# A bank emptied ahead of the next weights' split, rows of roots later, and a wider state-space table

## What is computed

```python
for l in range(2):
    h = h + 0.5 * swiglu(rmsnorm(h, ffn1_norm[l]), ...)          # hidden width 2816
    h = h + hybrid_mixer(rmsnorm(h, mix_norm[l]), w_in[l], ...)  # mLSTM, retention, gated delta rule
    h = h + 0.5 * swiglu(rmsnorm(h, ffn2_norm[l]), ...)
h = rmsnorm(h, final_norm)
hn = rmsnorm(h, norm1_w)                                         # second kind of block
gates, z, xbc, dt_raw, lru_x, lru_y = split(hn @ w_in)
y_ssm = mamba2_mixer(z, xbc, dt_raw, ...) @ w_out_ssm            # 4 groups of 8 heads, chunks of 128
y_lru = rglru_mixer(lru_x, lru_y, ...) @ w_out_lru               # width 1280, associative scan
h = h + (sigmoid(g_ssm) * y_ssm + sigmoid(g_lru) * y_lru) @ w_out
h = h + swiglu(rmsnorm(h, norm2_w), ...)
return rmsnorm(h, norm_f_w)
```

## Time and profile before

| | |
|---|---|
| median of 3 runs | 3571.42 us (3570.7 to 3572.22) |
| profiled execution | 3571.62 us; its span from first to last instruction 3569.5 us |
| TensorE matmuls busy | 3362.7 us, 94%, 15366 instructions |
| weight loads busy | 2724.7 us, 76%, beside the matmuls |
| VectorE busy | 1722.0 us, 48% |
| ScalarE busy | 1334.0 us, 37% |
| transfers | 288.05 MB, mean 81 GB/s |
| mean granted clock of TensorE | 0.978 |

### The profile page before, as it was taken

How to read it: one execution, slowest core, us unless ns; L and a number is a source line. 1 busy time by engine, 2 the same in 40 slices (tenths; PEclk the granted TensorE clock), 3 DMA queues, 4 the chain that set the end, 5 groups by cost and what they waited for, 6 DMA issues and landing times.

```text
span 3569.5 us, 38933 instructions
## 1 busy us (share of the span) xinstructions
PE 3362.7 (94%) x15366; PEld 2724.7 (76%) x15366; DVE 1722.0 (48%) x2415; ACT 1334.0 (37%) x1894; POOL 30.6 (1%) x62
## 2 busy tenths in 40 slices
PE   8999989899999999998989999989998998999998
PEld 6888766677888888876667788877777876778887
DVE  4443444754443444344575444455445566544443
ACT  4332335343332333233534332345444456433322
POOL 0000000000000000000000000000000000000000
PEclk9999999999999999999999999999999999999999
DMA  4233211112333233321111223321211222333332
GB/s 141 95 97 94 93 65 53 33 54 89 97 94 99 91 99 92 98 90 59 59 33 60 88 96 92 99 70 45 74 48 48 84 84 69 96 97 100 95 93 67
DMA packets 107396, 288.05 MB, mean 81 GB/s; under 512 B 22912, under 2 KB 34176, under 8 KB 107216
## 3 DMA queue, kind: packets, MB, share of 16 engines
q1 hardware_dynamic: 91696, 278.70, 25.0%
q10 hardware_dynamic: 14208, 2.63, 0.4%
q0 software_dynamic: 1312, 4.25, 0.4%
HBM read 282.64 MB, written 2.88 MB: 80 GB/s over the span
## 4 chain that ended last, share of the span: by engine, by line
PE 76%; DVE 12%; ACT 8%; issue 3%; ACTq 1%; DMA 1%; DVEq 0%; SPq 0%
PE ps L729 23%; PE ps L731 22%; PE ps L730 22%; DVE wl L1841 3%; ACT wh L1298 3%; DVE mf L2025 2%; PE ps L738 2%; PE ps L1038 1%; PE ps L1033 1%; PE ps L1194 1%; DVE mf L2035 1%; PE ps L1176 1%; PE ps L1190 0%; ACTq L1575 0%; PE ps L743 0%
## 5 line engine op out<-in xcount | busy, mean ns | idle before, releaser
L1841 DVE TENSOR_TENSOR wl<-raw,wh 128x1024 fp32r<-128x1024 f32 (+2 forms) x581 | 652.5, 1123 | 1448.0 <-ACT wh L1298 1446.2
L729 PE MATMUL ps<-hnh,wh 128*128 128x512 f32 x2712 | 1095.7, 404 | 38.4 <-DVE mf L2488 12.7
L730 PE MATMUL ps<-hnl,wh 128*128 128x512 f32 x2712 | 1070.6, 395 | 0.0
L731 PE MATMUL ps<-hnh,wl 128*128 128x512 f32 x2712 | 1070.1, 395 | 0.0
L1298 ACT ACTIVATE wh<-raw 128x1024 fp32r<-128x1024 f32 (+2 forms) x581 | 567.4, 977 | 1055.9 <-PE ps L731 1024.8
L729 PEld LDWEIGHTS ps<-hnh,wh 128*128 128x128 f32 x2712 | 519.3, 191 | 170.4 <-issue 24.5
L731 PEld LDWEIGHTS ps<-hnh,wl 128*128 128x128 f32 x2712 | 518.0, 191 | 111.4
L730 PEld LDWEIGHTS ps<-hnl,wh 128*128 128x128 f32 x2712 | 519.6, 192 | 108.3 <-issue 4.0
L729 PE MATMUL ps<-mr,wh 128*128 128x512 f32 x1300 | 511.7, 394 | 18.6 <-DVE h L1967 8.2
L731 PE MATMUL ps<-mr,wl 128*128 128x512 f32 x1300 | 507.0, 390 | 0.0
L730 PE MATMUL ps<-mr,wh 128*128 128x512 f32 x1300 | 506.8, 390 | 0.0
(11 more groups left out here) (324 smaller groups left out, 2533.0 us busy)
## 6 DMA issues: line engine op xcount, KB each, us to landing
raw<-in_w_in SPq DMA_DIRECT2D x140, 512.0 KB, 3.5
raw<-in_ffn_w_gate SPq DMA_DIRECT2D x88, 512.0 KB, 3.5
raw<-in_ffn_w_up SPq DMA_DIRECT2D x88, 512.0 KB, 3.5
raw<-in_ffn_w_down SPq DMA_DIRECT2D x64, 512.0 KB, 3.5
raw<-in_w_ffn_in SPq DMA_DIRECT2D x44, 512.0 KB, 3.5
raw<-in_ffn_w_down SPq DMA_DIRECT2D x32, 384.0 KB, 3.1
raw<-in_w_out SPq DMA_DIRECT2D x32, 256.0 KB, 2.6
raw<-in_w_out_ssm SPq DMA_DIRECT2D x32, 256.0 KB, 2.6
```

Source lines behind the costliest of these rows:

```text
L729: self.e.matmul(out, ah, bh, start=start, stop=False, skip_group_check=shared)
L730: self.e.matmul(out, ah, bl, start=False, stop=False, skip_group_check=shared)
L731: m = self.e.matmul(out, al, bh, start=False, stop=stop, skip_group_check=shared)
L1841: self.e.tensor_tensor(lo[:, 0:n], k.raw[u % NRAW][:, 0:n], hi[:, 0:n].bitcast(F), ALU.subtract).then_inc(k.w_lo, 1)
```

## The change

On VectorE `split` now only notes the unit; `flush` does the noted split. It is called behind the instruction that takes a product out of its bank in `add_h`, `ffn_up` and `take_mix`, at the beginning of each product and unit, ahead of each step, and when the next unit is to be split. The first units, in `start`, are split directly. `rstd` on TensorE now notes that the rows are due, and `rows_of` runs in the next product, ahead of its third input tile; in a round of fewer than eight input tiles `sums(0)` comes together with `sums(1)`. The state-space table has 45 steps instead of 43, other places, and other paces.

```diff
@@ constants
-PACE_SSM_ROWS, PACE_SSM, PACE_LRU, PACE_LRU_END = 1.1, (1.1, 0.82, 0.82, 0.9), 0.65, 1.0
+PACE_SSM_ROWS, PACE_SSM, PACE_LRU, PACE_LRU_END = 1.1, (1.15, 0.86, 0.86, 0.95), 0.65, 1.0
-SSM_STEPS, SCAN_STEPS = 43, 11
-AT_CB, AT_TURN, AT_X = (0, 2, 2, 3), (6, 8), 8
-AT_ARG, AT_EXP, AT_W, AT_V = 6, 7, 8, 12
-AT_ST, AT_OFF, AT_Y = 12, 12, 16
-AT_ROOT, AT_RESULT, AT_HIGH, AT_LOW = (30, 32, 34), (37, 37, 37, 37), (38, 39, 40, 41), (39, 40, 41, 42)
+SSM_STEPS, SCAN_STEPS = 45, 11
+AT_CB, AT_TURN, AT_X = (0, 2, 2, 3), (6, 10), (8, 9, 12, 13)
+AT_ARG, AT_EXP, AT_W, AT_V = 8, 9, 10, 14
+AT_ST, AT_OFF, AT_Y = 16, 16, 18
+AT_ROOT, AT_RESULT, AT_HIGH, AT_LOW = (32, 34, 36), (39, 39, 39, 39), (40, 41, 42, 43), (41, 42, 43, 44)
@@ Program
     def step(self):
+        self.flush()
         g = self.work.pop(0)
...
     def product(self, xs, ready, bank=None):
         b = B_PROJ[self.q % 2] if bank is None else bank
-        for _ in self.pieces(xs, ready, bank):
+        for n, _ in enumerate(self.pieces(xs, ready, bank)):
             self.beside()
+            if n == 1:
+                self.root_rows()
         return b
...
             i, self.late = self.late, None
-            if i >= 6:
-                self.sums(i - 6)
+            if i == 6 and not self.short:
+                self.sums(0)
             if i == 7:
+                if self.short:
+                    self.sums(0)
+                self.sums(1)
...
         self.r += 1
+        self.short = len(xs) < 8
@@ Tensor
         if self.r == OUT:
             return
-        self.wait_ge(*k.rs_v.at(self.rs_n(), "cols"))
-        self.rows_of(k.ps[B_RSTD], k.rc, k.rs_p.up(self.rs_n(), "rows"))
+        self.rows_due = self.rs_n()
+
+    def root_rows(self):
+        k, n = self.k, self.rows_due
+        if n is not None:
+            self.rows_due = None
+            self.wait_ge(*k.rs_v.at(n, "cols"))
+            self.rows_of(k.ps[B_RSTD], k.rc, k.rs_p.up(n, "rows"))
@@ Vector
     def split(self, u):
+        self.flush()
+        self.unsplit = u
+
+    def flush(self):
+        if self.unsplit is not None:
+            u, self.unsplit = self.unsplit, None
+            self.split_unit(u)
+
+    def begin_product(self, bank):
+        self.flush()
+
+    def begin_unit(self):
+        self.flush()
+
+    def split_unit(self, u):
         k = self.k
...
     def add_h(self, i, scale):
...
                                     op0=ALU.mult, op1=ALU.add).then_inc(k.took, 1)
+        self.flush()
         self.wait_ge(k.took, self.nv)
...   (the same flush behind the instruction with k.took in ffn_up and take_mix; start calls split_unit)
@@ Vector.ssm_heads
-            if AT_X <= t < AT_X + 4:
-                i = t - AT_X
+            if t in AT_X:
+                i = AT_X.index(t)
```

More of the change, by code:

```diff
@@ L182, in __init__ @@
         self.g_v = steps("g_v", in_order(
-            [(AT_X + i, f"x{i}") for i in range(4)], [(AT_ST + 2 + 4 * c, f"{n}{c}") for c in (1, 2) for n in "ds"],
+            four_at("x", AT_X), [(AT_ST + 2 + 4 * c, f"{n}{c}") for c in (1, 2) for n in "ds"],
             [(AT_OFF + 1 + 4 * c, f"m{c}") for c in range(1, 4)], [(AT_Y + 4 * c, f"y{c}") for c in range(1, 4)],
@@ L297, in __init__ @@
         self.gates_done, self.prepared = {}, []
+        self.short, self.rows_due, self.unsplit = False, None, None
         self.qk_took, self.v_took = {}, {}
@@ L345, in split @@
         pass
+    def flush(self):
+        pass
     def pieces(self, xs, ready, bank=None):
@@ L1848, in start @@
         self.hn_last = 0
-        self.split(0)
+        self.split_unit(0)
         self.wait_ge(k.loaded["col"], 16)
@@ L1853, in start @@
             if i == 1:
-                self.split(1)
+                self.split_unit(1)
             self.wait_ge(*k.hn_a.at(i, "hi"))
@@ L1862, in start @@
             if i in (5, 7):
-                self.split((i - 1) // 2)
+                self.split_unit((i - 1) // 2)
         self.wait_ge(k.loaded["cst"], 32)
```

## The result

The changed kernel took 3436.15 us, median of 4 runs (3432.48 to 3444.17), the kernel before 3571.56 beside it (3570.7 to 3572.22): a ratio of 0.9624, 95% interval 0.9605 to 0.9643.

A forecast was written before the change was run, and what follows sets the result against it. TensorE was taken as the bound, busy 94%, leaving 207 us of idling and slow-clock stretches. Terms 18 + 14 + 15 + 2.5 + 11 + 2 + 11 = 73.5 off 3571.6 gave 3498 us, range 3463 to 3543.

The forecast's parts named there:

- ends of the mixers: Last eight short products of each mixer: bank waits, the wait for first sums and slow matmuls go; 18 us, bounds 9 and 19.
- middles of the mixers and roots before them: Mixer middles: earlier evictions shorten about ten waits, 14 us, bounds 0 and 30; later root rows before mixers, 2 us.
- state-space groups and table: State-space groups: wider table and earlier evictions remove waits for the scaling and L2035; 11 us, bounds 0 and 18.
- recurrent unit: Recurrent unit: evictions come where VectorE's idling began, cutting waits for L2488 and L2385; 15 us, bounds 8 and 27.
- starts: First feed-forward eviction and first one of the second block no longer stand behind a split; 2.5 us, bounds 0 and 3.
- roots before feed-forward blocks: Four feed-forward starts: six matmuls of the next product run before the wait for root rows; 11 us, bounds 6 and 13.
- about ten of them behind such an eviction; the rest hang on chains of the delta heads in which the split is only one step: Mixer middles: of some 16 TensorE waits over 1 us, only about ten were counted, at 1.2 us each.
- Waits for L2035 (3.7 us) go, with the table below: State-space groups: the new eviction order was credited only with TensorE's 3.7 us of waits for L2035, booked with the table.
- A: Rival: the chains take gains back; mixer ends and roots stay (29), about 10 of the other 44; 3533 us, chance 0.22.
- B: Rival: everything goes, slow stretches vanish and convolutions start 1.9 us earlier in all 58 products; 3466 us, chance 0.14.
- C: Rival: low halves come too late where units are short, four-tile products and gates z; slower, 3597 us, chance 0.03.
- The rule by which an emptied bank does not break the clock: Rival from the Trainium skill: copying out of PSUM leaves TensorE's clock intact, so clock gains are nothing; 3514 us, chance 0.08.

The follow-up runs named there:

- d2_evict: The kernel before with only the splits postponed behind the evictions; table, sums and rows old: 3464.6 us, 0.9703.
- l2_lag_new: The changed kernel with VectorE's splits one unit later, on a high half made one product earlier: 3413.7 us, 0.9560.
- d3_rows: The kernel before with only the rows of reciprocal roots moved behind the first six matmuls of the next product: 3558.2 us, 0.9961.
- l1_lag_old: The kernel before, split still ahead of eviction, but VectorE splits a unit whose high half is a product old, except during gates z: 3458.5 us, 0.9688.
- l4_z: The changed kernel, but each split made at once while the state-space gates z are computed: 3443.5 us, 0.9638.
- c1_seam: The changed kernel with the postponed split flushed ahead of the last taps in `finish`, called only in the second block: 3429.2 us, 0.9605.

## Why the prediction was right in sign and too small

Against the profiled executions (127.2 us in all), each term of the sum:

| term | forecast | found |
|---|---|---|
| ends of the mixers | 18 | 23.2 |
| middles of the mixers and roots before them | 14 + 2 | 35.6 |
| state-space groups and table | 11 | 39.9 |
| recurrent unit | 15 | 12.0 |
| starts | 2.5 | 4.3 |
| roots before feed-forward blocks | 11 | 11.8 |

*Ends of the mixers*: right in mechanism. From the first to the eighth eviction 1.5 us went (28.2, now 26.7), which the forecast left out; in the last eight 6.2 (26.7, now 20.5), and 4.0 behind them. The forecast's cycle of 3.2 us measures 2.99. (The cuts between terms are evictions, and these now come earlier in TensorE's work, the first h tile's by 7 matmuls or 1.6 us in d2_evict; so much may belong to the neighbouring term.)

*Roots*: right. The six matmuls run first, four waits of 0.70 us are left of the six of 1.84 to 2.2 (forecast 0.85 at two places), and the mixers' starts give it back, as argued: the wait for L2002 at 411.11 became

```profile
407.97 0.51 PE L743 MATMUL ps<-hnh,wh 128*128 128x512 f32 x1 [3.25 <-DVE mf L2041]
```

*Recurrent unit*: right, L2488's 12.7 us fell to 2.2, and 5.2 us of L2385's 8.2 stayed.

*Middles of the mixers*: the step that failed is "about ten of them behind such an eviction; the rest hang on chains of the delta heads in which the split is only one step". I sized the gain by the waits of TensorE whose releaser stood behind a late eviction, at 1.2 us each, and gave the others nothing. But the split was not one step of those chains: at every unit VectorE stood idle for the high half with the chains' next steps queued behind it, 109.5 us in a mixer. Up to the first h tile the two mixers had 31 waits of over 1 us, 72.2 us together, and in d2_evict 20, of 41.8 us; the stretches became 40.8 us shorter. The wait of 6.59 us lost 3.6 (forecast 1.1 to 1.9), and waits for other steps shrank too: the one of 3.34 us for L2139 to 2.43, the one of 3.56 for ScalarE's L1613 to 2.62. The answer to the earlier trace rows in the trace of after shows what remained:

```profile
497.17 0.69 DVE L2074 TENSOR_TENSOR mf<-ps,mf 128x512 f32<-128x512 f32 x1 [1.54 <-PE ps L745]
500.75 1.23 DVE L1878 TENSOR_TENSOR wl<-raw,wh 128x1024 fp32r<-128x1024 f32 x1 [2.88 <-ACT wh L1319]
...
504.17 2.02 PE L1059 MATMUL ps<-mf,mf 128*128 128x512 f32 x4 [2.95 <-DVE mf L2312]
```

The wait of 6.59 us is 2.95 long. The 2.88 us of idling and the split still stand in front of the taps (from 501.89 on), though not all of that is their cost: the taps' input from ScalarE (L1453) was there only at 501.26. That the split's wait in front of VectorE's queue is the cause is shown from two sides: taken away in either order it gave 106 and 112 us, and work put there instead cost 65. Not shown is how its effect divides between evictions, with which each convolution's chain begins, and the other steps in the queue.

*State-space groups*: the same step failed more clearly, "Waits for L2035 (3.7 us) go, with the table below". The table was sized well (17.2 us in this part, 12.5 over the block; forecast 11, bounds 0 to 18). The eviction was given the 3.7 us that TensorE's list names, and took 24.0 in d2_evict: 1.9 at the block's start, 8.0 more up to the eviction of the sixth convolution (56.8 us after the block's root, now 46.9), and 14.1 in the groups behind it. About 3.4 of the 8.0 are the cut itself, for this eviction now comes 15 matmuls earlier in TensorE's work. Most of this first stretch lies ahead of 2392 us, where the forecast had no window, and no term but the first eviction; TensorE's wait of 5.2 us for L2035 in it stayed (5.0).

*Rivals.* A (the chains take it back) had the sign of this mechanism wrong: the chains were what gained. B (everything goes, 3466) came nearest and was still 30 us too slow; it counted convolutions that start earlier but no other step. C was seen in small, 8.2 us of waits for low halves behind z where 3.2 were before, not for want of 8.2 us of cover but, in the case shown, because three taps stood in front. The rule by which an emptied bank does not break the clock: TensorE was busy 35.9 us less here with the same 15366 matmuls, and 56 less in l2_lag_new (3306.5). The Trainium skill (TensorE: Matmul & The Clock Gate, Loop structure matters more than you think) says that copying a result out of PSUM does not break PE warmth. Where TensorE had to wait for the copy, this case shows a cost: behind the wait of 4.08 us for L2488 the first matmul took 0.50 us, against 0.39 at full clock.

*Range.* Its lower end was B's time less 3 us. All the bounds in it came from TensorE's waits and the part of each that an earlier eviction could reach, and the effect lay in waits for steps that had been given nothing.

*Luck.* That the terms for the recurrent unit (15, found 12.0) and for the roots (11, found 11.8) lie close is only in part the sizing: d3_rows alone gave 13 us, and the order alone gave 13.3 in the recurrent unit and 2.6 and 2.7 at the roots behind a mixer, so the same microseconds could be booked under more than one term.

## What to carry to other kernels

Where a helper engine waits for another engine at the head of its queue, read that engine's own waits by stage before sizing an edit that removes them: in the stages where its work is on the path, 305 us less of VectorE's wait for high halves (521.0, now 216.0 in d2_evict) gave 98 us, about a third, and in a feed-forward stage 105 us less (188.8, now 84.0) gave nothing. A wait between two engines that work in step can be removed by taking the input one unit older as well as by reordering around it (112 and 106 us here), and the two together gave 22 us more than the changed kernel. An experiment that is to part two causes needs a number for each: l1_lag_old was meant to leave the bank late, and only the trace shows that it did not. And an edit at a helper such as the one that ends the taps must be followed to all its callers before it is read as a test of one place.

## What the runs showed beyond that

Some of the new kernels scatter more from execution to execution than the old: 3432 to 3444 us for after, 3430 to 3448 for l4_z and 3417 to 3442 for c1_seam, against 3569.3 to 3577.7 in 15 runs of before; l2_lag_new (3411 to 3416) does not. Within one execution of after the two mixers, which run the same program of steps, took 399.4 and 391.2 us (424.5 and 424.8 before); 346.5 and 338.3 of these lie ahead of the first h tile, the rest is equal to 0.1 us. What differs there was not tested. Differences of a few microseconds in one mixer, between two profiled executions, therefore carry little.
